# Expert down projection with both parts of the rows side by side as 128 weight columns, and an add on VectorE

## What is computed

```
y[token] = sum over the 2 experts e chosen for the token of weight * expert_block(x, e)

def expert_block(args):
    xb, e = args                       # 64 rows of 1024
    hid = jax.nn.silu(xb @ w_gate[e]) * (xb @ w_up[e])      # 64 x 512
    return hid @ w_down[e]                                  # 64 x 1024
```

## Time and profile before

| | us |
|---|---|
| median of 3 runs | 1688.06 |
| lowest, highest | 1685.96, 1688.34 |
| profiled execution, time | 1685.04 |
| profiled execution, span | 1683.3 |
| first to last down projection of the experts | 472.9 to 1005.0 |

### The profile page before, as it was taken

The page is one execution under the profiler, slowest core; times in us unless marked ns, Lnnn a source line. Parts: engine busy times, 40 slices in busy tenths (PEclk is TensorE's granted clock), DMA queues, the critical chain, the costliest instruction groups (busy, mean ns, idle before and its releaser), DMA issues.

```text
span 1683.3 us, 19172 instructions
## 1 busy us (share of the span) xinstructions
PE 1481.1 (88%) x6513; PEld 1078.9 (64%) x6514; DVE 921.3 (55%) x1040; ACT 733.0 (44%) x847; POOL 250.4 (15%) x260
## 2 busy tenths in 40 slices
PE   7899988698099999999999987989799999969969
PEld 6788754445076767677777663544378788858746
DVE  6833144403488989888888843371644223431543
ACT  4433222201378888888888840241033212321120
POOL 1011000013322332223222210140000000000030
PEclk8999867798599999999999997999899999979979
DMA  5222510032099999999999978200012222232201
GB/s 202 78 73 100 183 68 1 18 99 100 7 349 383 390 388 385 385 390 386 382 383 388 378 220 256 101 1 26 0 50 100 100 100 97 87 116 95 81 7 44
DMA packets 135651, 294.42 MB, mean 175 GB/s; under 512 B 18238, under 2 KB 20396, under 8 KB 135596
## 3 DMA queue, kind: packets, MB, share of 16 engines
q1 hardware_dynamic: 122812, 270.64, 44.4%
q10 hardware_dynamic: 7168, 14.59, 2.4%
q0 software_dynamic: 5616, 8.44, 1.6%
HBM read 289.67 MB, written 12.88 MB: 180 GB/s over the span
## 4 chain that ended last, share of the span: by engine, by line
PE 63%; DVE 16%; issue 9%; ACT 5%; DMA 3%; DVEq 2%; POOL 1%; SPq 0%; ACTq 0%; POOLq 0%
PE ps L791 10%; PE ps L812 10%; PE ps L459 7%; DVE ring_r L1731 7%; PE ps L616 6%; PE ps L571 3%; PE ps L765 3%; PE ps L844 3%; PE ps L650 3%; PE ps L414 2%; PE ps L643 2%; ACT hi L1292 2%; PE ps L503 2%; PE ps L672 2%; PE ps L538 1%
## 5 line engine op out<-in xcount | busy, mean ns | idle before, releaser
L1731 DVE TENSOR_TENSOR ring_r<-ring,hi 128x2048 fp32r<-128x2048 f32 x192 | 427.0, 2287 | 53.7 <-ACT hi L1292 53.5
L1292 ACT ACTIVATE hi<-ring 128x2048 fp32r<-128x2048 f32 x192 | 356.2, 1907 | 2.1 <-DMA ring<-in_w_gate 2.0
L1471 DVE TENSOR_TENSOR ring_r<-ring,ring_r 128x4096 fp32r<-128x4096 f32 x25 | 110.6, 4426 | 174.5 <-ACT ring_r L1162 174.5
L812 PE MATMUL ps<-ring_r,ats 128*128 128x512 f32 x768 | 177.6, 394 | 4.0 <-DVE ats L1861 3.2
L812 PEld LDWEIGHTS ps<-ring_r,ats 128*128 128x128 f32 x768 | 146.2, 191 | 35.4 <-issue 4.8
L1162 ACT ACTIVATE ring_r<-ring 128x4096 fp32r<-128x4096 f32 x25 | 90.5, 3620 | 167.8 <-PE ps L812 132.3
L1018 POOL TENSOR_TENSOR rsv<-msv,half 128x1 f32<-128x1 f32 (+2 forms) x32 | 32.8, 1027 | 833.1 <-DVE msv L1431 833.1
L616 PE MATMUL ps<-ring_r,XTS 128*128 128x512 f32 x512 | 130.7, 398 | 5.9 <-issue 4.1
L616 PE MATMUL ps<-hi,XTS 128*128 128x512 f32 x512 | 127.6, 392 | 0.0
L650 PE MATMUL ps<-hi,HIDS 128*64 128x512 f32 x512 | 125.3, 397 | 0.0
L791 PE MATMUL ps<-ring_r,ring_r 128*128 128x512 f32 x512 | 121.4, 389 | 1.8 <-DVE hi L1849 1.8
(11 more groups left out here) (286 smaller groups left out, 1939.8 us busy)
## 6 DMA issues: line engine op xcount, KB each, us to landing
ring<-in_w_gate SPq DMA_DIRECT2D x32, 2048.0 KB, 13.4
ring<-in_w_up SPq DMA_DIRECT2D x32, 2048.0 KB, 16.2
ring<-in_w_down SPq DMA_DIRECT2D x32, 2048.0 KB, 14.5
ring<-in_w_ff SPq DMA_DIRECT2D x16, 2048.0 KB, 8.2
ring<-in_w_in SPq DMA_DIRECT2D x8, 2048.0 KB, 9.1
X<-in_x ACTq DMA_DIRECT2D x8, 512.0 KB, 5.0
ring<-in_w_out SPq DMA_DIRECT2D x2, 2048.0 KB, 7.6
M<-results ACTq DMA_DIRECT2D x8, 512.0 KB, 7.2
```

Of the source, the lines that this page charges most:

```text
L812: ins = pe.matmul(ps[:, 2 * t + c, :], ATS[a][:, 4 * (n % 4) + k, t * P:(t + 1) * P], w[b][:, k, c * 512:(c + 1) * 512], start=(n % 4 == 0 ...
L1292: act.activation(HI[u][:, c], ring[:, s, c], ACT.Copy).then_inc(w_hi, 1)
L1471: vec.tensor_tensor(ring_r[s][:, :], ring[:, s, :], split_hi[j % 2][:, :].bitcast(F32), ALU.subtract).then_inc(s_lo, 1)
L1731: vec.tensor_tensor(ring_r[s][:, c], ring[:, s, c], HI[u][:, c].bitcast(F32), ALU.subtract).then_inc(w_lo, 1)
```

## The change

In the down projection the two parts of HIDS lie side by side as 128 weight columns (its layout is now f, part, row). Each of the weights' rest and top is passed over once: 8 matmuls each, 16 in place of 24. The result of the hi part is in partitions 0 to 63 of banks 4 and 5, that of the lo part in 64 to 127. (The product of lo part and rest, which the kernel before leaves out, is now in the sum.) ScalarE copies partitions 64 to 127 into the new buffers `YL`, one for each bank, and VectorE adds them to partitions 0 to 63 into `YB`. The two adds stand in VectorE's order between the lo halves of up and those of down. TensorE now waits for both parts of HIDS before its first matmul. `y_left`, for which TensorE's next down projection and GpSimd's scatter wait, is now given by VectorE's adds; the new semaphore `y_rest_out` goes from ScalarE to VectorE.

```diff
+        YL = [m(a, 512)[0:BLK] for a in (1024, 15360)]
-        HIDS = as_r("HIDS", M_AT + 14720, 2, FT, BLK)
+        HIDS = as_r("HIDS", M_AT + 14720, FT, 2, BLK)
+        y_rest_out = sem("y_rest_out")
@@ TensorE
-                until(pe, hid_hi, g + 1)
                 w_rest = ring_r[raw[2]][:, :].rearrange("p (k c) -> p k c", k=FT)
                 w_top = HI[2][:, :].rearrange("p (k c) -> p k c", k=FT)
+                until(pe, hid_ready, g + 1)
                 for c in range(2):
                     for f in range(FT):
-                        ins = pe.matmul(ps[0:BLK, 4 + c, :], HIDS[:, 0, f, :], w_rest[:, f, c * 512:(c + 1) * 512],
-                                        start=(f == 0), stop=False)
+                        ins = pe.matmul(ps[:, 4 + c, :], HIDS[:, f, :, :].rearrange("p s b -> p (s b)"),
+                                        w_rest[:, f, c * 512:(c + 1) * 512], start=(f == 0), stop=False)
                 ins.then_inc(down_raw_used, 1)
-                until(pe, hid_ready, g + 1)
                 for c in range(2):
-                    for a in range(2):
-                        for f in range(FT):
-                            ins = pe.matmul(ps[0:BLK, 4 + c, :], HIDS[:, a, f, :], w_top[:, f, c * 512:(c + 1) * 512],
-                                            start=False, stop=(a == 1 and f == FT - 1))
+                    for f in range(FT):
+                        ins = pe.matmul(ps[:, 4 + c, :], HIDS[:, f, :, :].rearrange("p s b -> p (s b)"),
+                                        w_top[:, f, c * 512:(c + 1) * 512], start=False, stop=(f == FT - 1))
                     ins.then_inc(y_full, 1)
@@ ScalarE
-                act.activation(HIDS[:, 0, :, :], HIDG, ACT.Copy).then_inc(hid_hi, 1)
+                act.activation(HIDS[:, :, 0, :], HIDG, ACT.Copy).then_inc(hid_hi, 1)
...
-                    act.activation(YB[:, c, :], ps[0:BLK, 4 + c, :], ACT.Copy).then_inc(y_left, 1)
+                    act.activation(YL[c], ps[BLK:P, 4 + c, :], ACT.Copy).then_inc(y_rest_out, 1)
@@ VectorE
-                vec.tensor_tensor(HIDS[:, 1, :, :], HIDG, HIDS[:, 0, :, :].bitcast(F32), ALU.subtract).then_inc(hid_ready, 1)
+                vec.tensor_tensor(HIDS[:, :, 1, :], HIDG, HIDS[:, :, 0, :].bitcast(F32), ALU.subtract).then_inc(hid_ready, 1)
                 rows_lo(g + 1)
                 if ahead:
                     weights_lo(e + 1, 0, 1 - odd, 1)
-                    for u in range(1, 3):
-                        for half_ in range(2):
-                            weights_lo(e + 1, u, 1 - odd, half_)
+                    for half_ in range(2):
+                        weights_lo(e + 1, 1, 1 - odd, half_)
+                for c in range(2):
+                    vec.wait_ge(y_rest_out, g * 2 + (c + 1))
+                    vec.tensor_tensor(YB[:, c, :], ps[0:BLK, 4 + c, :], YL[c], ALU.add).then_inc(y_left, 1)
+                if ahead:
+                    for half_ in range(2):
+                        weights_lo(e + 1, 2, 1 - odd, half_)
```

## The result

| | before | after |
|---|---|---|
| median in the comparison, us | 1687.01 | 1815.86 |
| lowest, highest of after, us | | 1809.88, 1819.09 |
| ratio, 95% interval | | 1.077 [1.074, 1.079] |
| profiled execution: time, span | 1685.04, 1683.3 | 1819.09, 1817.2 |

What follows compares the result with a forecast made beforehand. VectorE's chain was taken to bound most expert blocks: 29 intervals +27.4 us, less 1.5, 0.2 and 0.7, together +25.0, giving 1710.0 profiled, 1713.1 on the median, stated as 1711.5 us; range 1706 to 1716, widened to 1702 to 1728.

Steps and rivals of the forecast that it cites:

- VectorE's block and the adds: Expert stage: two adds cost 1.30 us and lengthen VectorE's block from 16.41 to 17.71 us, 29 intervals +27.4 us.
- lower bound of 1.22: VectorE's two adds: least cost 1.22 us, with 0.08 us overlap; upper bound 1.38, taken 1.30.
- the thirtieth interval: End of the loop, 959 to 983 us: a 24.3 us interval set by TensorE, forecast to lose 1.5 us.
- TensorE: not the bound: Down projection: 16 matmuls take 3.7 us, making a TensorE block of 14.6 us against VectorE's 17.71.
- the clock rival: Same as rival 1: TensorE becomes the bound by its low clock, 1735 us; chance 0.14.
- rival 1: TensorE's low clock decides from 6.7 us per block; 8.5 us gives 18.5 us blocks, +23 more, 1735; chance 0.14.
- The stream: Weight stream by DMA: a 17.71 us block needs 363 GB/s, below the present 386, so no limit.
- GpSimd: the step that failed: Later y_left: scatter lands 1.1 us into the next block, gathered rows at 12.1, wanted about 15.5; 3 us cover.
- 6.8 and 7.4 us "to landing": GpSimd: the scatter takes 6.8 us to land, the gather queued behind it 7.4.
- My list of signs: Expected marks in the profile after; a rows_in wait ahead of the transposes would mean GpSimd's cover was too thin.
- Rivals 2 and 3: VectorE's adds: 2, taken into idle time, about 1681 (chance 0.05); 3, cheaper and partly hidden, within 0.2% (0.07).
- rival 2: Expert stage: TensorE and stream set the pace, long blocks shrink to 16.7 us, about 1681; chance 0.05.

Runs made afterwards that it cites:

- gather first: Changed kernel with GpSimd's wait for the scatter's landing and pick of its row numbers moved behind the next gather; 1705.47 us (1.012).
- adds alone: Kernel before plus two same-size VectorE adds into scratch at the changed kernel's place, y_left still early from ScalarE's copies; 1708.03 us (1.014).
- one pause: Changed kernel with VectorE waiting for its own second add ahead of the first lo half of the down weights; 1712.28 us (1.016).
- the runs with small adds: Changed kernel plus a one-column add behind each lo half of the down weights, with or without a PSUM operand; 1794.25 and 1795.23 us (both 1.062).

## Why the forecast was wrong, step by step

**VectorE's block and the adds: right.** 17.59 us, against 17.71 in the forecast and 16.41 in the earlier trace rows. Groups of after, of 470 to 1140:

```profile
L1082 POOL DMA_INDIRECT results<-M,idx x32 | 117.1, 3660 | 117.9 <-DVE M L1755 113.4 <-issue 4.6
...
L645 PE MATMUL ps<-ring_r,HIDS 128*128 128x512 f32 x256 | 111.8, 608 | 39.9 <-DVE HIDS L1747 39.9
L1076 POOL DMA_INDIRECT M<-h_rows,idx x31 | 86.5, 2792 | 26.7 <-POOL idx L1072 25.8 <-DVE M L1755 0.9
...
L1755 DVE TENSOR_TENSOR M<-ps,M 64x512 f32<-64x512 f32 x64 | 40.9, 675 | 4.9 <-ACT M L1320 4.9
```

An add takes 675 ns against the 692 of L1736 in the earlier trace rows, and two start to start with their follower take 1.20 (698.56 to 699.76), not 1.30: the overlap of the earlier trace rows holds for them, and my lower bound of 1.22 was the better value. They hardly wait for ScalarE's copies (4.9 us in all). The three kernels in which the rows come in time, gather first, adds alone and one pause, give 1705.5, 1708.0 and 1712.3: the forecast of 1711.5 is within 6 us of the time of this change without the mechanism that it missed. The two largest terms that put it above the first of them are the block (29 x 0.12 = 3.5 us) and the thirtieth interval, for which I took 1.5 us off; it fell from 24.3 to 17.6, in after too. Why it is so long in before I can't say from these runs.

**TensorE: not the bound, as forecast, but 3.7 us was the time at the full clock only; the clock rival half right.** The 16 matmuls stand behind a longer wait (2.63 us ahead of L645). The engine then works at its lower level more than before: the granted clock is 0.50 from 707.8 to 711.6, 0.54 from there to 713.0 and 1.00 behind, so that the 16 take 6.3 us, and the window from 492 to 1108 has a clock of 0.83 against 0.97 in the earlier trace rows. In the short blocks this changes nothing, they stay at 17.59: what rival 1 put as its point of decision, 6.7 us of low clock in a block, isn't reached by the some 5 us seen.

**The stream: not the limit, as forecast.** It runs at 307 GB/s, less than the 363 of the forecast because of the long blocks; in the kernel that gathers first, with 17.59 in every block, it is 370 (480 to 1000).

**GpSimd: the step that failed.** I put the scatter at t0 + 11.1, its landing 1.1 us into the next block and the gathered rows at 12.1, with 3 us to spare. In the block of the timelines, with t0' = 706.36 for the start of the next block, it went so:

```
                               forecast      measured                    late by
scatter landed                 t0' +  1.1    712.30 = t0' +  5.9         4.8
from there to gather's issue   3.6           717.44 - 712.30 = 5.1       1.5
from there to rows in          7.4           731.15 - 717.44 = 13.7      6.3
rows in                        t0' + 12.1    731.15 = t0' + 24.8        12.7
```

TensorE wanted them at 723.2, 16.9 into the block, so there were 4.8 us of cover, and 12.7 - 4.8 = 7.9 us are left: the wait at L607. In nine other long blocks it is the copy of the row numbers that takes the 7.4 to 7.7 us, and the gather's issue follows it late. In a long block VectorE stands still, GpSimd's next issue goes through in 0.93 us, and the rows after it come in time. Hence the turn of short and long.

The mistake was to take the 6.8 and 7.4 us "to landing" of the earlier trace rows as the time of a transfer that can be moved anywhere. They are medians that hold an issue by GpSimd as it lay in before. The copies of row numbers I had in the 3.6 us between, also as they lay in before. That its length was not a constant could be read in before, in lines that I hadn't shown and that stand next to those of the earlier trace rows (timeline of GpSimd in before):

```profile
714.32 2.09 POOL L1082 DMA_INDIRECT results<-M,idx  x1 [4.60 <-ACT M L1320]
...
725.65 2.80 POOL L1076 DMA_INDIRECT M<-h_rows,idx  x1 [0.88 <-POOL idx L1072]
731.94 0.93 POOL L1082 DMA_INDIRECT results<-M,idx  x1 [3.49 <-ACT M L1320]
```

Two lengths for the same instruction, 0.93 where VectorE has a pause and 2.09 where it doesn't, and for the gather 0.97 and 2.80: the longer ones end 0.87 to 0.93 us behind a border between two operations of VectorE. I should have asked what they would be in a row of half tiles without a pause. One half tile more for each, about 2.2 us, is a bound that the earlier trace rows would have given; the cover of 3 us less twice 2.2 is below nothing, and this step would have been the leading rival and not a sentence. The rest of the size, three half tiles and not one, was in no row of before. My list of signs did name a wait for rows ahead of the transposes as the mark of a cover too thin; that is what came.

The Trainium skill has a mechanism of this kind, on its page "SBUF — State Buffer", section "SBUF: two separate sides": VectorE and GpSimd share a pair of ports to SBUF, which one of them holds alone until its instruction ends; a VectorE operation with two SBUF inputs, as the half tiles are, takes it only against a GpSimd operation that reads SBUF. I hadn't weighed it. The page puts the end of such a wait about 115 ns behind the end of VectorE's operation. The runs agree that GpSimd waits for the end of an operation of VectorE: copies that were held end 0.04 us behind it, and issues 0.87 to 0.93 us behind the start of the next, which is about what an issue takes with nothing in its way (0.93). They differ in that here the hold went on over several operations (6.52 us for operations of 2.28, and copies held across five borders). That it is these ports that hold GpSimd is argued and not shown: no run takes an SBUF input away from the half tiles.

**Rivals 2 and 3** (VectorE takes the adds for nothing; adds cheaper than any row) fell with the adds alone, +23 us. What rival 2 said of TensorE's share was tested by itself: the long blocks do shrink, and the stream of 385 GB/s takes it back.

**What stays open.** Why short operations directly ahead of a row of half tiles put VectorE in the manner of 70 to 80 ns, in which GpSimd is mostly kept out. It isn't the operand in PSUM or how long the adds are, and how long the data had been ready doesn't fit either; a pause of 0.13 us ends it. That a queue ahead of the engine is filled by short operations, and emptied by a pause, would fit; no run here tests it. That the shorter overlap and the holding have one cause is also read from their going together, and not shown.

## What to carry to other kernels

When a change moves an issue of GpSimd in time, look at what VectorE does at the new place, and price the issue as one that may last until VectorE's next pause. A group whose mean duration lies between two values of the same instruction is a warning; here 0.93 and 2.09 became 6.52. Where such a chain (result, scatter, pick, gather, transposes) has only a few microseconds of cover, take the scatter out of it first (its landing and its row numbers, not its issue): that alone was worth 110 us here, and a pause of VectorE at the right place 104.

## What the runs showed of the hardware

- GpSimd's issue of a transfer of 64 rows takes 0.92 to 0.98 us when VectorE pauses, 1.1 to 3.1 when one operation of VectorE is in its way, and up to 7.7 (7.9 in the runs with small adds) when it isn't let in. A copy of 64 numbers by GpSimd is held as well: up to 2.3 us behind one operation, and 7.4 to 7.7 in nine blocks of after, in place of 0.18.
- Operations of VectorE start 70 to 87 ns before the recorded end of the one before, and the two ends of that range (below and above about 80) go with two behaviours toward GpSimd: above, it always got in; below, it was mostly kept out.
- A wait of VectorE for its own last operation costs 0.2 us between two operations (blocks of 17.80 against 17.59; the engine idles 0.12 to 0.23), and about 2 us where it is the last of VectorE's work in a block.
- 128 weight columns cost TensorE the same as 64 for each matmul; but in the block shown the eight behind 2.6 us of idle time ran at half the clock (0.50 in the window 707.8 to 711.6), so that 16 matmuls took 6.3 us (707.82 to 714.09) where 24 at the full clock take 5.5 (24 x 0.230).
